# Two layer norms between matmul stages: worked by token halves, with one chunk moved to ScalarE

## The reference, cut to what matters

```python
def layer_norm(x, g, b):
    xf = x.astype(jnp.float32)
    mu = xf.mean(-1, keepdims=True)
    var = jnp.square(xf - mu).mean(-1, keepdims=True)
    return ((xf - mu) * lax.rsqrt(var + LN_EPS) * g + b).astype(x.dtype)

x = layer_norm(ALPHA * x + hybrid_mixer(x), ln_g[0], ln_b[0])          # norm 0
x = layer_norm(ALPHA * x + mem_cross_attention(x), ln_g[1], ln_b[1])   # norm 1
x = layer_norm(ALPHA * x + swiglu(x), ln_g[2], ln_b[2])                # norm 2
# second block: starts with rmsnorm(x, norm_g) and x @ w_in
```

## Time and profile before

| | |
|---|---|
| median of 3 runs | 2252.07 us (2250.58 to 2252.34) |
| profiled execution | 2250.64 us, its span 2248.8 us |
| mean granted clock of PE | 0.998 |
| PE busy | 2231.8 us, 99% of the span |
| DVE busy | 1307.9 us, 58% |
| ACT busy | 1038.8 us, 46% |
| POOL busy | 173.0 us, 8% |
| chain that ended last, by engine | PE 96%, DVE 2%, POOL 1% |

### The profile page before, as it was taken

How to read it: one execution, slowest core, us unless ns; L and a number is a source line. 1 busy time by engine, 2 the same in 40 slices (tenths; PEclk the granted TensorE clock), 3 DMA queues, 4 the chain that set the end, 5 groups by cost and what they waited for, 6 DMA issues and landing times.

```text
span 2248.8 us, 29509 instructions
## 1 busy us (share of the span) xinstructions
PE 2231.8 (99%) x10256; PEld 1849.3 (82%) x10256; DVE 1307.9 (58%) x1571; ACT 1038.8 (46%) x1239; POOL 173.0 (8%) x175
## 2 busy tenths in 40 slices
PE   9999999999999999999999999999999999999999
PEld 8888888888888788888888888877888888888887
DVE  5555655566667854454445545566666656645674
ACT  4444445545444444433444344435445454445643
POOL 1000000001203210000000000003000000200020
PEclk9999999999999999999999999999999999999999
DMA  7755654556755365656655565555566665765554
GB/s 234 227 174 164 185 159 159 189 163 213 263 177 198 123 230 181 197 190 193 192 189 187 187 197 186 192 172 159 161 194 197 195 194 171 218 186 174 168 188 167
DMA packets 216454, 421.29 MB, mean 187 GB/s; under 512 B 15240, under 2 KB 19376, under 8 KB 214448
## 3 DMA queue, kind: packets, MB, share of 16 engines
q1 hardware_dynamic: 212928, 401.79, 56.5%
q0 software_dynamic: 3168, 17.82, 2.4%
q10 hardware_dynamic: 272, 0.52, 0.1%
HBM read 417.97 MB, written 2.11 MB: 187 GB/s over the span
## 4 chain that ended last, share of the span: by engine, by line
PE 96%; DVE 2%; POOL 1%; DMA 0%; ACT 0%; issue 0%; ACTq 0%; SPq 0%; DVEq 0%
PE b_ps L571 90%; PE b_ps L599 1%; PE b_ps L616 1%; PE b_ps L668 1%; DVE b_w_lo L1479 1%; PE b_ps L683 1%; POOL b_x_res L499 1%; DVE b_x_res L1630 0%; DVE b_x_res L1639 0%; PE b_ps L677 0%; PE b_ps L759 0%; PE b_ps L736 0%; POOL b_x_res L510 0%; POOL b_x_res L505 0%; PE b_ps L684 0%; DMA b_gate_a<-in_x 0%
## 5 line engine op out<-in xcount | busy, mean ns | idle before, releaser
L1479 DVE TENSOR_TENSOR b_w_lo<-b_stage,b_w_hi 128x1024 fp32r<-128x1024 f32 (+1 forms) x762 | 935.2, 1246 | 618.1 <-ACT b_w_hi L1065 615.3
L1065 ACT ACTIVATE b_w_hi<-b_stage 128x1024 fp32r<-128x1024 f32 (+1 forms) x762 | 794.5, 1054 | 685.2 <-PE b_ps L571 656.7
L571 PE MATMUL b_ps<-b_w_hi,b_x_hi 128*128 128x512 f32 (+1 forms) x2364 | 938.5, 397 | 0.7 <-DVE b_w_lo L1479 0.5
L571 PE MATMUL b_ps<-b_w_hi,b_x_lo 128*128 128x512 f32 (+1 forms) x2364 | 921.0, 390 | 0.0
L571 PE MATMUL b_ps<-b_w_lo,b_x_hi 128*128 128x512 f32 (+1 forms) x2364 | 919.4, 389 | 0.0
L571 PEld LDWEIGHTS b_ps<-b_w_hi,b_x_lo 128*128 128x128 f32 x2364 | 444.5, 188 | 93.6
L571 PEld LDWEIGHTS b_ps<-b_w_hi,b_x_hi 128*128 128x128 f32 x2364 | 445.0, 188 | 92.2 <-issue 3.2
L571 PEld LDWEIGHTS b_ps<-b_w_lo,b_x_hi 128*128 128x128 f32 x2364 | 445.2, 188 | 87.6
L571 PE MATMUL b_ps<-b_w_hi,b_ff_h 128*128 128x512 f32 x352 | 137.3, 390 | 0.0
L571 PE MATMUL b_ps<-b_w_hi,b_ff_l 128*128 128x512 f32 x352 | 137.0, 389 | 0.0
L571 PE MATMUL b_ps<-b_w_lo,b_ff_h 128*128 128x512 f32 x352 | 136.9, 389 | 0.0
(11 more groups left out here) (294 smaller groups left out, 1462.3 us busy)
## 6 DMA issues: line engine op xcount, KB each, us to landing
b_stage<-in_w_in SPq DMA_DIRECT2D x335, 512.0 KB, 4.2
b_stage<-in_w_ffn_in SPq DMA_DIRECT2D x176, 512.0 KB, 4.5
b_stage<-in_w_ffn_out SPq DMA_DIRECT2D x88, 512.0 KB, 4.1
b_stage<-in_w_out SPq DMA_DIRECT2D x64, 512.0 KB, 4.0
b_stage<-in_w_up SPq DMA_DIRECT2D x24, 512.0 KB, 4.1
b_stage<-in_w_o_dsa SPq DMA_DIRECT2D x16, 512.0 KB, 4.7
b_stage<-in_w_o_moba SPq DMA_DIRECT2D x16, 512.0 KB, 4.3
b_stage<-in_w_kv_mem SPq DMA_DIRECT2D x16, 512.0 KB, 3.5
```

Of the source, the lines that this page charges most:

```text
L571: ins = mm(ps[:, ACC + r, 0:n], x[:, kt + t, rows], w[:, slot, t, 0:n], start=first and t == 0 and k == 0, stop=last and t == GK - 1 and k ...
L1065: act.activation(w_hi[:, slot, :, 0:n], stage[:, slot, :, 0:n], ACT.Copy)\
L1479: dve.tensor_tensor(w_lo[:, slot, :, 0:n], stage[:, slot, :, 0:n], w_hi[:, slot, :, 0:n].bitcast(F32), ALU.subtract).then_inc(sem("lo_done ...
```

## The change

In norms 1 and 2 (norm 0 keeps its arrangement):

- The block before the norm ends with its last two groups taken together (`two_groups`): first both groups for token half 0, then both for half 1, so that half 0 is complete 12 matmuls ahead of the end rather than six. The first two groups after the norm are taken in the same way.
- DVE adds, measures and norms chunk 0 for half 0 (`rows_normed`), then adds half 1, makes `x_lo` for half 0's batches 0 and 1, and does the same for half 1. It has no part in chunk 1 any more. A small operation more gives `shift` = -mean/std.
- ACT centres and scales chunk 1 of both halves in one operation each (bias `shift`, scale `rstd`), and half 1 of chunks 2 and 3. Chunk 1 is turned without its weight and bias, into two PSUM banks that are free there (`SC` and `PT`). ACT adds weight and bias on the way out of them, where they are one number for each partition (`ln_gc`, `ln_bc`), into `nat`, and then makes `x_hi` of `nat`; DVE makes `x_lo` of `nat`.
- The weights and biases as columns come by four new loads, behind that of `g_col`; POOL multiplies the ones of norm 2 by `g_col` before norm 0.
- POOL centres and scales half 0 alone of chunks 2 and 3, weighs all of them, chunk 2 first, and last of all chunk 1, whose natural form is needed much later.
- `LN_FILL` is now four throw-away runs of 3, 6, 3 and 4 turns (the fifth number isn't used). Before it was 19 and 15.
- Squares in norm 2 are taken in the order of chunks 0, 2, 3, 1.

```diff
-LN_FILL = (19, 15)
+LN_FILL = (3, 6, 3, 4, 5)
+        def bank_of(t, normed):
+            return (SC, PT)[t - 2] if normed and t in (2, 3) else TP + t % 2
...
+            for m in (1, 2):
+                load(ln_gc[:, m - 1, :], a["ln_g"][m, :].rearrange("(t p) -> p t", p=P), "small2",
+                     allow_slow_non_contiguous=True)
+                load(ln_bc[:, m - 1, :], a["ln_b"][m, :].rearrange("(t p) -> p t", p=P), "small2",
+                     allow_slow_non_contiguous=True)
...
+                    pool.wait_ge(sem("norm_ready"), 2 * m)
+                    for n in (2, 3):
+                        centre_scale(n, 0)
+                    for n in (2, 3):
+                        pool.wait_ge(sem("pool_step"), c.value("pool_step"))
+                        weigh(n, 0)
+                        pool.wait_ge(sem("scaled"), 3 * m - 3 + n)
+                        weigh(n, 1).then_inc(sem("late_chunk"), 1)
+                    pool.wait_ge(sem("tp_done"), c.at(f"turned{m}"))
                     for r in range(R):
+                        ins = weigh(1, r)
                     ins.then_inc(sem("late_chunk"), 1)
...
+            def two_groups(kt, first, last, hi, lo, ready=None):
+                slot = c.value("g") % SLOTS
+                for r in range(R):
+                    for i in range(2):
+                        if ready:
+                            ready(r, i)
+                        if r == 0:
+                            pe.wait_ge(sem("lo_done"), c.next("lo_done"))
+                        half_group((slot + i) % SLOTS, r, kt + i * GK, first and i == 0, last and i == 1, hi, lo)
+                c.next("g", 2)
...
+                def rows_ready(r, i):
+                    if i == 0:
+                        keep_warm(LN_FILL[2 * r])
+                        for t in range(2):
+                            pe.wait_ge(sem("chunk"), 4 * m + 2 * r + t)
+                            turn_rows(t, r).then_inc(sem("tp_done"), 1)
+                        c.next("tp_free", 2)
+                        if r == 1:
+                            pe.wait_ge(sem("scaled"), 3 * m - 2)
+                            for t in (2, 3):
+                                for row in range(R):
+                                    ins = turn_rows(t, row)
+                                ins.then_inc(sem("tp_done"), 1)
+                            c.next("tp_free", 2)
+                        keep_warm(LN_FILL[2 * r + 1])
+                    pe.wait_ge(sem("tp_free"), fed + 2 * r + i + 1)
+                two_groups(0, True, False, x_hi, x_lo, ready=rows_ready)
+                for j in range(2, KT // GK):
+                    pe.wait_ge(sem("tp_free"), fed + 4 + j - 1)
+                    group(j * GK, False, j == KT // GK - 1, x_hi, x_lo)
+                    if j + 2 < KT // GK:
+                        if j % 2 == 0:
+                            pe.wait_ge(sem("late_chunk"), 3 * m - 1 + j // 2)
+                        feed_batch(x_res, j + 2)
...
-                weights(kts=4, hi=om_h, lo=om_l, before=merged_heads)
+                weights(kts=4, hi=om_h, lo=om_l, before=merged_heads, rows_last=b == 3)
...
+                act.wait_ge(sem("ln_cols"), 2)
+                for t in (2, 3):
+                    act.wait_ge(sem("tp_done"), c.next("tp_done"))
+                    for k, at in enumerate(columns(t)):
+                        act.activation(nat[:, t - 2, k * S:(k + 1) * S], ps[:, bank_of(t, True), k * S:(k + 1) * S],
+                                       ACT.Identity, bias=ln_bc[:, m - 1, at], scale=ln_gc[:, m - 1, at])
...
+            def norm_and_feed(m, i, alpha, vecs, scale=None):
+                residual(i, alpha, True, (0,))
+                rows_normed(0, vecs)
+                residual(i, alpha, False, (1,))
+                for t in range(2):
+                    lo_rows(t, 0, scale)
+                statistics(i, 1)
+                rows_normed(1, vecs)
+                for t in range(2):
+                    lo_rows(t, 1, scale)
+                split()
+                for t in (2, 3):
+                    scaled_batch(t)
+                split()
```

More of the change, by code:

```diff
@@ L856, in _ @@
             x_fed = c.value("tp_free")
[L857 removed]
+            chunk_of = first_normed()
             def feed_x(batches):
@@ L1126, in after @@
                     if hook:
                         hook(j)
-                weights(hook=after)
             def root(x):
@@ L1394, in _ @@
                 if n == 0:
-                    feed_weights(x_hi, g_col, squares)
+                    feed_normed(2, g_col, squares)
                     root(rms[:, :])
@@ L1610, in gated_at, with residual @@
                     c.next(f"tile_out{r}")
-            def residual(i, alpha, stat):
+            def residual(i, alpha, stat, rows=range(R)):
                 cols = ds(i * NB, NB)
-                for r in range(R):
+                for r in rows:
                     tile_done(r)
@@ L1660, in norm_chunk @@
                 centre(cols)
-                rescale(cols)
+                rescale(cols).then_inc(sem("chunk"), 1)
             for name in TOKENS["dve"]:
@@ L1951, in _ @@
                 weights(kts=4)
-                residual(b, ALPHA, True)
-            norm_root(96)
+                if b < 3:
+                    residual(b, ALPHA, True)
             def hidden(feeding=False, hook=None):
                 if feeding:
-                    feed_weights(x_hi, x_lo, norm=norm_chunk)
+                    norm_and_feed(1, 3, ALPHA, 96)
                 else:
@@ L2018, in _ @@
                 if n == 0:
-                    feed_weights(x_hi, x_lo, g_col, norm_chunk)
+                    norm_and_feed(2, 3, 1.0, 128, g_col)
+                    forget_weights()
                     dve.wait_ge(sem("squares"), 8)
```

271 lines of the change are left out of this document (188 added, 83 removed).

## The result

The changed kernel took 2256.2 us (median of 8 runs, 2254.61 to 2259.35) against 2251.47 for the kernel before (8 runs as well): a ratio of 1.0021, with a 95% interval of [1.0011, 1.0031]. It is a little slower, where 0.5% faster was forecast. The profiled span is 2253.0 us, 4.2 more than before.

A forecast was written before the change was run, and what follows sets the result against it. PE was taken to bound the kernel, on the chain for 96% of the span, so only its standstills could be won. 7.3 + 7.6 - 0.8 - 3.3 = 10.8 us gave a median of 2241.3, range 2235.5 to 2249.

The forecast's parts named there:

- Everything else at nothing. The pause-free rest is untouched.: Outside the norms and column loads: no cost; norm 0 the same, POOL's small products and `vec` loads in long pauses.
- Norm 1, gain 7.3: Norm 1: group 3 starts at 781.9 instead of 789.15, DVE's 6.72 us on chunk 1 gone; 7.3 us won.
- Norm 2, gain 7.6: Norm 2: group 4 starts at 1529.1 against 1536.7 in effect, after 1.5 us of standing; 7.6 us won.
- Rival 3: Both norms: ACT is the bound, its added operations costing 3 us more in each norm; 2247, chance 0.09.
- Rival 2: Norms 1 and 2: POOL's operations take 2.26 instead of 1.7, batch 6 late, 6.8 us go; 2248, chance 0.09.
- The clock, 0.8 lost: Norm 1: half 0's matmuls run at PE's reduced clock after the wait, now on the path; 0.8 us lost.
- Column loads, 3.3: At 593 to 601 us: 8192 more separate pieces delay the weights and PE waits; 3.3 us lost.
- Rivals 1 and 4: Column loads cost 5 us or a little more (2243.0, chance 0.20), or hold the queue 40 us (2257, chance 0.07).
- The estimate of 5.4 us: Column loads by the skill's 10.5 ns a packet, 512 more on each of 16 engines: the sum 2.1 us later.
- the forecast of 2241.3: Whole kernel: the forecast median after 10.8 us won, against 2252.07 before; chance 0.50.

The follow-up runs named there:

- e2_before_32b: The kernel before with filler `align` 8 floats longer, so all tiles behind it lie 32 bytes further: 2262.6 us, ratio 1.0046.
- e1_aligned: The changed kernel with filler `align` shortened by 32 bytes, so later tiles lie at their old addresses: 2242.99 us, ratio to before 0.9959.
- e6_no_weigh: The changed kernel, tiles at old addresses, column loads issued earlier, POOL weighing 8 of 512 columns in norms 1 and 2: 2236.61 us.
- e7_batch4_first: The changed kernel, tiles at old addresses, column loads earlier, batch 4's `x_hi` and `x_lo` made before group 5's split: 2239.87 us.
- e3_before_cols: The kernel before with the four new column loads alone, used by nobody: 2253.92 us, ratio 1.0008.

## Why the prediction was wrong, step by step

- **"Everything else at nothing. The pause-free rest is untouched."** This is the step that failed. The instructions were the same, but 2,040 matmuls of that rest took 6.2 ns more each: 12.6 us by that product, 11.8 us by matching the matmuls, 12.2 us in the trace of e2_before_32b (10.6 by the medians), 13.2 us by e1_aligned against the changed kernel (2256.2 - 2242.99). It turns the sign. The diff showed it: the line `align` was in it, with R floats taken off for a tile that takes 32 bytes. Neither the edit nor its price had a place in the sum or the rivals.
- **Norm 1, gain 7.3.** At group 3 it was 7.3, as forecast, and the first matmul came 3.1 us behind the old block (3.5 forecast). But 1.8 us more are lost ahead of group 4, so 5.5 are left. What failed is the price of DVE's splits, 1.2 us each in the sum and 2.2 beside POOL's multiplications and additions.
- **Norm 2, gain 7.6.** 8.5 were forecast at group 2, and 7.5 came: half 1's rescale took 1.89 us beside POOL instead of 0.87. Then came 1.38 us of waiting for group 3's split and 1.75 for batch 4's `x_lo`: 4.4 left. The last wait I had expected (1.5 us, for the squares' sake, which e6_no_weigh shows), the others I hadn't. Without POOL's two-input operations (e6_no_weigh) the two norms win 7.75 and 7.16 us, together the 14.9 of the forecast. So what the sum had wrong in the norms is what DVE and POOL cost each other.
- **Rival 3, "if these operations cost 3 us more in each norm, everything behind group 2 moves", with matmuls waiting for `b_w_lo`.** Its marker came, and part of its price: PE stood 2.0 and 3.1 us. The chain does begin at ACT's split for group 3 (784.40 in norm 1), but then it is DVE for 6.54 us, and e6_no_weigh shows that this is for POOL's two-input operations: ACT isn't the bound. I had charged POOL's presence to POOL and to half 1's norm, and had left DVE's splits at 1.2 us.
- **Rival 2, POOL late.** PE never waited for POOL in the norms of the changed kernel, but only because it had waited for DVE before. POOL's operations did take 2.2 us, and it ended chunk 3 of norm 1 22.3 us behind the old block (at 795.38) where 20.3 was forecast; PE turned batch 6 at 795.53. In e7_batch4_first, where the wait for DVE in front of it was gone, PE waited for POOL.
- **The clock, 0.8 lost.** Nothing was lost. In both norms half 0's matmuls run at a granted clock of 1.00, where it was 0.60 in the earlier trace rows. These are the windows of norm 2 and norm 1 (columns as there):

```profile
1520.40:1523.30 2.90, 2.83 (x12) 2.31 (x13) 2.79 (x10) 2.01 (x4) 2.82 (x3) 1.00 0.00 0
776.20:779.07 2.87, 2.87 (x13) 2.31 (x13) 2.77 (x9) 2.13 (x4) 2.87 (x2) 1.00 0.02 6
```

- **Column loads, 3.3.** 2.3 to 2.5 us in three traces (the changed kernel, e1_aligned and e3_before_cols). The mechanism was right: ACT waits for the weights, its splits are late, PE stands. Rivals 1 and 4 fell. The estimate of 5.4 us, worked out from the packet figure in the Trainium skill's "DMA: Bandwidth & Descriptors" ("Measured") and read as the rate of each of the 16 engines, was too high by more than a factor of two. The loads could be had for nothing in another place.

Summed as the matched matmuls have it: 5.5 + 4.4 won, 11.8 and 2.3 lost, and 0.2 of drift, 4.4 us slower; the spans show 4.2, the medians 4.7. Without the placement, the forecast of 2241.3 compares with 2242.99 measured, and that it is so near is partly luck: in that run's trace the norms won 5.3 us less than forecast, the clock and the loads cost 1.7 less, and its median lies 9.1 us under the kernel before where its trace has 6.6.

The Trainium skill's page "SBUF — State Buffer" has, in "SBUF: two separate sides", the rule that a VectorE operation with two SBUF inputs and a GpSimd operation take one pair of ports in turn, each for its whole length. Beside POOL's multiplications and additions the traces agree: splits 2.2 instead of 1.2, `x_lo` from `nat` 1.75 and from PSUM, with one SBUF input, 0.68. `x_lo` from `nat` took only 0.68 at 782.92 in the changed kernel, where it began just ahead of POOL's L523 (at 783.00), which then took 1.75 instead of 1.40. Beside POOL's centring (L515, from 774.46 to 779.06 in the changed kernel) VectorE isn't held up for a whole operation: L1776 has two inputs in SBUF and took 0.78 at 777.52, against 0.74 at 773.29, ahead of it. The prediction had this from a pair that took 0.87 beside L499. In the kernel before another such pair took 1.22, and the centring itself was slower beside splits, 6.68 us for two instead of 4.70, while the splits kept their 1.2 us each:

```profile
770.73 4.70 POOL L499 TENSOR_SCALAR b_x_res<-b_x_res,b_mv,b_rstd 128x512 f32<-128x512 f32 x2 [74.13 <-DVE b_rstd L1653]
771.47 1.22 DVE L1630 SCALAR_TENSOR_TENSOR b_x_res<-b_x_res,b_mv,b_vec_a 128x256 f32<-128x256 f32 x2
781.71 6.68 POOL L499 TENSOR_SCALAR b_x_res<-b_x_res,b_mv,b_rstd 128x512 f32<-128x512 f32 x2
782.19 2.35 DVE L1479 TENSOR_TENSOR b_w_lo<-b_stage,b_w_hi 128x1024 fp32r<-128x1024 f32 x2
```

The same section says of PE that it never waits on anyone. No run here speaks against that, but PE's two operands did disturb each other.
